# The expert stage is begun in a stage of its own between the two halves, and picks come in the first twelve parts of a head pair

## What is computed

```python
def one_block(xb):
    q = rms_norm((xb @ wq).reshape(blk, P_HEADS, P_QDIM), qn_w)            # 8 heads, 256 each
    s1 = jnp.einsum('thd,hnd->thn', q[..., :P_HALF], k1)                   # 128 keys
    s2 = jnp.einsum('thd,hnd->thn', q[..., P_HALF:], k2)                   # 128 keys
    v1, i1 = lax.top_k(s1, P_TOPK); v2, i2 = lax.top_k(s2, P_TOPK)         # 16 each
    cand = (v1[..., :, None] + v2[..., None, :]).reshape(blk, P_HEADS, P_TOPK * P_TOPK)
    sc, sel = lax.top_k(cand, P_TOPK)                                      # 16 experts of 16384
    g = jax.nn.softmax(sc, axis=-1)
    act = jax.nn.gelu(jnp.einsum('td,thkd->thk', xb, u[eidx]))
    return jnp.einsum('thk,thkd->td', (g * act), v[eidx])
```

## Time and profile before

| | us |
|---|---|
| median of 3 runs (lowest, highest) | 5161.5 (5159.6, 5164.9) |
| the profiled execution, whole | 5164.3 |
| its span (what the rows cover) | 5162.6 |

### The profile page before, as it was taken

One profiled execution on the slowest core, in us unless ns is written; L12 is line 12 of the kernel. 1 busy time (PEld: TensorE's weight loads), 2 busy tenths in 40 slices (PEclk: granted clock), 3 DMA queues, 4 the chain that ended last, 5 costly groups with the idle time before them and its releaser, 6 DMA issues. The chain is left out here.

```text
span 5162.6 us, 43530 instructions
## 1 busy us (share of the span) xinstructions
PE 3510.0 (68%) x13217; PEld 1859.7 (36%) x13217; DVE 2785.9 (54%) x7544; ACT 1378.0 (27%) x4604; POOL 1563.8 (30%) x1191
## 2 busy tenths in 40 slices
PE   4999666665699997875434677769655555555556
PEld 2768553542443345543212244536211111111111
DVE  2350433345445533757665664344677777777775
ACT  1111331012325422322222222032332333332332
POOL 2545000133211121214443332011343444434443
PEclk7999577877799998667777667879777777777778
DMA  5543134368677776559988999466899999999998
GB/s 184 179 155 125 36 106 134 98 204 324 249 269 268 270 287 236 215 214 321 332 317 322 412 385 355 170 235 205 324 417 401 417 415 407 412 414 410 416 413 366
DMA packets 428509, 1473.86 MB, mean 285 GB/s; under 512 B 40785, under 2 KB 166641, under 8 KB 293074
## 3 DMA queue, kind: packets, MB, share of 16 engines
q0 software_dynamic: 152064, 1107.36, 53.6%
q1 hardware_dynamic: 261842, 356.51, 20.7%
q10 hardware_dynamic: 14368, 7.21, 0.5%
HBM read 1403.58 MB, written 74.57 MB: 286 GB/s over the span
## 5 line engine op out<-in xcount | busy, mean ns | idle before, releaser
L2304 PE MATMUL expert_acc<-uv_ring,diag 128*64 128x512 f32 x4096 | 1374.0, 809 | 990.3 <-ACT diag L2249 890.7
L2117 POOL DMA_INDIRECT uv_ring<-in_peer_uv,pick_idx x1056 | 1181.2, 1119 | 2535.5 <-PE expert_acc L2304 1776.6
L2223 DVE SCALAR_TENSOR_TENSOR uv_ring<-uv_ring,n_pairs 128x1024 f32<-128x1024 f32 x1056 | 1278.1, 1226 | 446.3 <-DMA uv_ring<-in_peer_uv,pick_idx 445.1
L2304 PEld LDWEIGHTS expert_acc<-uv_ring,diag 128*64 128x64 f32 x4096 | 316.7, 171 | 1933.4 <-ACT diag L2249 1304.4
L2249 ACT ACTIVATE diag<-half_pattern,pick_weight 128x64 f32<-128x64 f32 x1024 | 298.5, 338 | 598.3 <-DVE pick_weight L2192 587.3
L2258 ACT ACTIVATE gelu_cube<-dots_now 128x2 f32<-128x2 f32 x528 | 106.0, 201 | 1101.7 <-DVE uv_ring L2223 1063.8
L559 PE MATMUL h_acc_q<-in_w_all_q,n_all_q 128*128 128x512 f32 (+1 forms) x800 | 353.5, 597 | 0.0
L2190 DVE SCALAR_TENSOR_TENSOR gelu_now<-gelu_tanh,dots_now 128x2 f32<-128x2 f32 x528 | 85.1, 161 | 380.4 <-ACT gelu_tanh L2261 303.8
L2261 ACT ACTIVATE gelu_tanh<-gelu_cube,dots_now 128x1 f32<-128x1 f32 x1056 | 253.2, 286 | 16.2
L556 PE MATMUL h_acc_q<-n_all_q,in_w_all_q 128*128 128x272 f32 x896 | 213.0, 397 | 18.9 <-DMA in_w_all_q<-in_w_in 18.9
L559 PEld LDWEIGHTS h_acc_q<-in_w_all_q,n_all_q 128*128 128x128 f32 (+1 forms) x800 | 135.7, 174 | 216.5 <-issue 216.5
(11 more groups left out here) (417 smaller groups left out, 5044.8 us busy)
## 6 DMA issues: line engine op xcount, KB each, us to landing
in_w_p<-in_w_in SPq DMA_DIRECT2D x34, 1024.0 KB
in_w_all_q<-in_w_in SPq DMA_DIRECT2D x17, 2048.0 KB
ada_w<-in_w_ada SPq DMA_DIRECT2D x12, 2048.0 KB, 9.3
q_broadcast_q<-qk_rows_dram SPq DMA_DIRECT2D x24, 1024.0 KB, 17.5
uv_ring<-in_peer_uv,pick_idx POOLq DMA_INDIRECT x1056
past_keys_q<-in_cache_kv_g SPq DMA_DIRECT2D x16, 1024.0 KB, 15.7
past_rows_q<-in_cache_kv_g SPq DMA_DIRECT2D x16, 1024.0 KB
score_pair<-scores SPq DMA_DIRECT2D x66, 128.0 KB
```

The costliest lines, as they stand in the source:

```text
L2117: pool.indirect_dma_start(self.ring[:, 2 * slot + s, :], None, self.x["peer_uv"][0], bass.IndirectOffsetOnAxis(ap=self.idx[:, q % 2, s, k: ...
L2223: ins = dve.scalar_tensor_tensor(out=row, in0=row, scalar=1.0, in1=self.n2[:, tile % 2, s if tile < LAST_TILE else 0, :], op0=ALU.mult, op ...
L2304: ins = pe.matmul(self.acc[s * 64:(s + 1) * 64, c, :], self.diag[:, part % DIAGS, s, :], rows, start=first, stop=last)
```

## The change

`Opening` is gone. `query_phase` of half p runs alone, then a new phase `experts_start` runs (the loads, the picks of group 0 and the first part's gathers), and then half q with `Beside`, now for turns 0 to 233. `experts_rest` takes turns 234 and on. By the order of POOL's instructions the 528 parts' gathers now stand so (before in brackets): query phase of p 0 (25), start 1, first norm 6 (5), projection 64 (61), hgrn 28 (26), attention 31 (28), merge 72 (67), branch 4 (4), output 5 (4), second norm 6 (6), queries of q 18 (17), rest 293 (285).

The picks of the next group move from turns 4 to 15 to turns 0 to 11, and the loads of scores move to turn 12, for the group after the next. In half p `query_phase` has three accumulators for its query product, before two.

```diff
-    SLOTS = 2
+    SLOTS = 2 if span.samples else 3
...
-class Opening(Alone):
-    FROM = {3: 0, 4: 2, 5: 7, 6: 12, 7: 18, 8: 24}
...
-    def after_head(self, name, h):
-        if h == 2 and name in self.begin:
-            self.begin[name]()
-        if h in self.FROM:
-            for i in range(self.FROM[h], self.FROM[h + 1]):
-                self.turn[name](i)
...
     def sp_start(self):
...
+        for s in range(2):
+            self.load_scores(1, s)
...
-        if i < N_PARTS and i % TOPK == 2:
+        if i < N_PARTS and i % TOPK == 12:
             for s in range(2):
-                self.load_scores(i // TOPK + 1, s)
+                self.load_scores(i // TOPK + 2, s)
...
-        if q + 1 < N_GROUPS and r >= 4:
-            self.pick(q + 1, (r - 4) // 6, (r - 4) % 6)
+        if q + 1 < N_GROUPS and r < 12:
+            self.pick(q + 1, r // 6, r % 6)
...
+def experts_start(nc, ph, experts):
+    block = ph.block()
+    @block.sync
+    def _(sp):
+        experts.sp_start()
+    @block.vector
+    def _(dve):
+        experts.dve_start()
+    @block.scalar
+    def _(act):
+        experts.act_start()
+    @block.gpsimd
+    def _(pool):
+        experts.pool_start()
...
-FRONT_PARTS = 242
-FRONT_US = 2010.8
+FRONT_PARTS = 234
+FRONT_US = 2011.0
...
-        front(SPANS[0], Alone(), False, opening)
-        beside = Beside(later[0], FRONT_PARTS, FRONT_US, Opening.FROM[PH])
-        front(SPANS[1], beside, True, None)
+        front(SPANS[0], Alone(), False)
+        experts = Experts(nc, keep, bank, const, x, dram, y_p[0], y_s.rearrange("b t d -> (b t) d"))
+        phase(experts_start, "_start", True, experts)
+        beside = Beside(experts, FRONT_PARTS, FRONT_US)
+        front(SPANS[1], beside, True)
```

More of the change, by code:

```diff
@@ L1684, in query_phase, with heads @@
     block = ph.block()
-    def heads(query, norm, rest, after):
+    def heads(query, norm, rest):
         query(0, 0)
@@ L1696, in heads @@
             rest(h)
-            after(h)
     @block.sync
@@ L1767, in _ @@
         split(0)
-        heads(query, lambda h: None, rest, lambda h: beside.after_head("pool", h))
+        heads(query, lambda h: None, rest)
     @block.tensor
@@ L1812, in rest @@
                 beside.pe(C_S)
-        heads(query, norm, rest, lambda h: beside.after_head("pe", h))
+        heads(query, norm, rest)
     @block.vector
@@ L1848, in rest @@
                 beside.dve(C_S)
-        heads(query, norm, rest, lambda h: beside.after_head("dve", h))
+        heads(query, norm, rest)
     @block.scalar
@@ L1878, in rest @@
                 beside.act(C_S)
-        heads(query, norm, rest, lambda h: beside.after_head("act", h))
+        heads(query, norm, rest)
 class Alone:
@@ L2413, in build, with front @@
         consts_phase(nc, lambda name: nc.alloc_semaphore(name=name), const)
-        def front(span, beside, busy, opening):
+        def front(span, beside, busy):
             T, N = span.count, len(span.tiles)
@@ L2451, in front @@
                           (kv1_p, kv2_p, kv3_p), (kv1_s, kv2_s, kv3_s))
-                with ExitStack() as last:
-                    if not busy:
-                        n_hi, n_lo = both(last, "n2", "right")
-                    with ExitStack() as rows:
-                        x1 = held(rows, "x1_held", [P, N, D], side="right")
-                        phase(out_phase, tag, busy, span, beside, const, x, dram, x_rows, mix, x1)
-                        late.close()
-                        if busy:
-                            n_hi, n_lo = both(last, "n2")
-                        phase(norm_phase, tag + "2", busy, span, beside, const, x["norm2_w"], dram["mod"], 3 * D, 4 * D, n_hi, n_lo, None, x1, n2_rows)
-                    phase(query_phase, tag, True, span, opening() if opening else beside, const, x, dram, n_hi, n_lo)
```

43 lines of the change are left out of this document (15 added, 28 removed).

## The result

| | before | changed |
|---|---|---|
| median of 20 runs each, us (lowest, highest) | 5157.2 (5142.6, 5174.1) | 5176.3 (5155.7, 5193.6) |
| ratio of the medians | | 1.0035, 95% interval 1.0024 to 1.0047 |
| span of the profiled execution, us | 5162.6 | 5168.3 |

The changed kernel is slower by 0.35%, about 18 us. The forecast was 20 us faster, and the time lies just above the range (5114 to 5175).

What follows compares the result with a forecast made beforehand. It took the rest, merge and attention as at or near the DMA limit, the projection as PE-bound, other stages as chains of waits. Terms -83 + 56 + 13 - 6 = -20 us gave 5141 us; own range 5125 to 5157, with rivals 5114 to 5175.

Steps and rivals of the forecast that it cites:

- query phase of p, start stage: Half p's query phase, run alone, gains 109.3 us; the bare start stage costs 26 us: -83 us.
- 16 parts in the front: Sixteen parts moved into half q's front stages, priced stage by stage between 1.94 and 4.91 us each: +56 us.
- the start stage's trace in the front: Effect of the start stage on half q's front stages behind it; the sum gave it no cost.
- picks in the front: In the merge of half q, 5 waits for `pick_idx` go, 4 to 5 of them worth 1.5 us: -6 us (0 to -9).
- 8 parts in the rest: Eight parts moved from half p's query phase to the rest stage, at about 5.1 us each: +40 us.
- picks in the rest: Moved picks end the `pick_idx` waits at group starts in the rest, 1.55 us a group: -27 us.
- without it 2.7: Recurrence of half q: without the sample tokens' section (some 60 us) a part costs 2.7 us, so two cost 5.4.
- work that now lies bare: The start stage between half p's queries and half q, costed at its own length: 26 us (24 to 30).
- rival 1: Half q's front has no cheap places: parts cost 5.21 us, front 83 instead of 56, total 5174 us; chance 0.15.
- rival 3: At group starts the ring, not `pick_idx`, starves the DMA engines: 27 + 6 us not won, total 5174 us; chance 0.10.
- next in line is the free slot of the ring [...] without harm to the DMA engines: In the rest, after the picks' waits go, POOL waits for ring slots, as already for 452.3 us, harmlessly.
- Rival 2: Half q's front has room: parts cost only their matmuls, 31 us instead of 56, total 5116 us; chance 0.15.

Runs made afterwards that it cites:

- e10: The kernel before, unchanged, profiled a second time; 5157.3 us in a single execution.
- e6: The changed kernel with 218 parts in front of half q instead of 234, so 16 more fall to the rest; 5199.8 us, ratio 1.0073 to the kernel before.
- e5: The kernel before with the moved picks alone, no start stage; groups 0, 1 and 15 keep the old places; 5133.6 us, ratio 0.9955.
- e11: The kernel of e5, unchanged, profiled a second time; 5123.1 us in a single execution.
- e2: The changed kernel with POOL holding back the gathers in half q's first norm until the norm's modulation rows have landed; 5163.0 us, ratio 1.0004 to the kernel before.
- e9: The changed kernel with e2's hold at the norm and 242 parts in front of half q instead of 234; 5138.9 us, ratio 0.9958 to the kernel before.
- e1: The changed kernel again, unchanged, profiled on the chip of e2 to e4; 5171.4 us, ratio 1.0028 to the kernel before.
- e4: The changed kernel with the picks put back to turns 4 to 15 and the score loads to turn 2; 5191.1 us, ratio 1.0056 to the kernel before.
- e3: The changed kernel with the recurrence's pace 1.38 instead of 1.5 (26 parts there, not 28) and 231 parts in front; 5182.6 us, ratio 1.0040 to the kernel before.
- e12: The changed kernel with 242 parts in front of half q instead of 234, without a hold at the norm; 5149.7 us, ratio 0.9972 to the kernel before.

## Why the prediction was wrong

The changed kernel against the mean of before and e10, with what the experiments say of each term:

| term | forecast | measured | from |
|---|---|---|---|
| query phase of p, start stage | -83 | -90 | windows |
| 16 parts in the front | +56 | +63 | changed against e6 |
| the start stage's trace in the front | 0 | +33 | e6 against e5 and e11 |
| picks in the front | -6 | -11 | e5 and e11 against before and e10 |
| 8 parts in the rest | +40 | +42 | e2 against e9 |
| picks in the rest | -27 | -14 to -21 | e5, e11; changed, e1, e2 against e4 |
| sum | -20 | +16 to +23 | the runs: +18 |

1. **The query phase and the start** came as worked out: stores 22.3 us apart, start 23.1 us. The term was 7 us too cautious: the phase took 181 us and not 185, the start stage with its barrier 24 and not 26. (The end at 1160.2 instead of 1170 is half due to an earlier begin.) That reading of SP's queue was right.
2. **The prices of the parts** were near in the sum: 3.9 us in front (forecast 3.5), 5.3 to 5.5 in the rest (5.21, later 5.11). Stage by stage they were not, and the sum is near partly by luck. The changed kernel against e6 has the same picks and the same start: the norm took 3.4 us more for its part (3.6 forecast), the projection 7.7 for 3 (5.8), attention 7.3 for 3 (12) and the merge 25.3 for 5 (24.6). The recurrence took 24 for 2 (5.4; 17 by e1's profile), and branches, output and queries together got 4 us shorter where 4.4 more were forecast. The step "without it 2.7" rests on 60 us for the sample tokens' section, which no run shows by itself. It fits when the parts come evenly (e3, e9, e12). It left out that whole parts are issued at a few places in a chain, and that a third part at a place has no gather in flight.
3. **The step that failed** is that the start stage was costed at its own length alone, "work that now lies bare", and its effect on the stages behind it at nothing; the runs show 33 us there. The prediction named the burst of gathers in rival 1 (as a delay for loads on SP's queue), and the sum priced the norm's one part at 3.6 us. The norm grew by 19, of which e2 gives 15 back. The query phase's cover did not only hide 24 parts; it also handed a nearly full ring to half q. Another 17 us of the front go with the start stage and stay unexplained.
4. **The picks** do what was forecast at the group starts (all windows at 424 GB/s or more, no wait), so rival 3 falls. The term was 6 to 13 us too large, because "next in line is the free slot of the ring [...] without harm to the DMA engines" was wrong at four places: the tile changes now lose 16 us where they lost 2. In the front the gain is there, but not where it was forecast. The 6 us were to come from the merge; there the waits for `pick_idx` are gone and the stage is no shorter (447 us in e5 and e11, 444 before), while the queries (11), the branches (7) and the output (3) got shorter and the recurrence 10 longer, by the means of two profiles each.
5. **Rival 1** gave nearly the measured time (5174 against 5176) for a partly wrong reason. By its own point, 4.7 us a part in front, it should not have decided: the parts cost 3.9 by e6. With the burst and the rest of the 33 us laid upon the 16 parts, though, it is 6 us a part. Rival 2's sum falls with e6, though its price, 1.94 us a part, is what the eight further parts of e12 cost.

Slower had been given a chance of 0.19. The start stage, the two parts in the recurrence and the picks were each priced where they stand, and what they did to the ring and the queues behind them was left out.

## What to carry over

When work is taken out from between two stages, ask what state the next stage used to inherit from it. Here it was a nearly full ring; the empty one cost 15 of the 90 us gained, and one wait gave them back in the norm (12 in the whole). A constant that was fitted to the old placing (how many parts go in front, at what pace) is part of the change: 242 for 234 alone turned 1.0035 into 0.9972, and with the hold and a shifted pace it is 0.9930. Test the parts of a joint change apart, since here one alone gained 23 us and hid behind the other.

## What the runs showed of the hardware

- Ten gathers of 128 rows x 8 KB (10.5 MB), issued in 12 us into idle DMA engines, doubled DVE's wait for 21 loads of another queue (2.9 MB): 36.7 us against 18.8, and 18.6 with the gathers held back. In 16 us of it the two queues moved 583 and 612 packets.
- The DMA engines moved 424 to 429 GB/s in the undisturbed windows that were read, of 8 to 40 us, nearly all of it gathers (16 of 1.05 MB in the 40 us window, 419 of 426 GB/s).
- How far the ring bridges a stop of POOL can't be told from the stop's length. At changes of tile a stop of 9.6 us left 385 GB/s in the worst 4 us (e10), one of 9.5 us left 199 (e5), and the last one in e10, of 11.6 us, left 376. Ahead of e10's two stops ten gathers had been issued in 12 to 13 us, ahead of e5's in 21.
- The length of a chain of short steps (the recurrence) varied between two profiles of one kernel by up to 11 us, while full stages (projection, merge) repeated within 1 us.
